# Two transformer blocks with a 32-expert mixture on one core: x read by tiles, weight splits issued at other places, and expert transfers cut in pieces at both ends of the experts

## The reference

```python
for l in range(2):                                   # block 1
    proj = rms_norm(x, norm_mix_pre[l]) @ w_in[l]    # 12 slices of 256 columns
    y = [conformer conv (31 taps), stick-breaking attention, retention, short gated conv]
    x = x + rms_norm(concat(y) @ w_out[l], norm_mix_post[l])
    x = x + rms_norm(conv_ffn(rms_norm(x, norm_ffn_pre[l]), ffn_up[l], ffn_conv_w[l], ffn_down[l]), ...)

mod = silu(c) @ ada_w + ada_b                        # block 2: shifts, scales and gates
u, uc = modulate(rmsnorm(x, norm1_g), ...), modulate(rmsnorm(ctx, norm1_g), ...)
y = token mixer of u, uc: chunked mLSTM (4 heads) and differential attention (8 heads),
    gated branches w_branch_a, w_branch_b, then w_out
x = x + g1 * y
v = modulate(rmsnorm(x, norm2_g), sh2, sc2)
top 4 of softmax(v @ router_w + router_b) over 32 experts; expert e of its tokens:
    h = v @ w1[e] + b1[e]                            # 1024 -> 2048
    a = min(h_glu, 7) * sigmoid(1.702 * ...) * (clip(h_lin, -7, 7) + 1)
    out = a @ w2[e] + b2[e]                          # 1024 -> 1024, summed with the gates
return rmsnorm(x + g2 * sum, final_norm_g)
```

## Time and profile before

| | |
|---|---|
| median of 3 runs | 2085.42 us (2079.37 to 2086.78) |
| the profiled execution | 2082.96 us, span 2081.1 us |
| granted clock, mean | 0.984 |
| PE busy | 1992.8 us, 96% of the span |
| DVE, ACT, POOL busy | 902.9, 633.2, 10.1 us |
| HBM read | 587.27 MB |
| chain that ended last | PE 78%, DMA 14%, DVE 4%, ACT 3%, issue 1% |

### The profile page before, as it was taken

One profiled execution on the slowest core, in us unless ns is written; L12 is line 12 of the kernel. 1 busy time (PEld: TensorE's weight loads), 2 busy tenths in 40 slices (PEclk: granted clock), 3 DMA queues, 4 the chain that ended last, 5 costly groups with the idle time before them and its releaser, 6 DMA issues.

```text
span 2081.1 us, 26818 instructions
## 1 busy us (share of the span) xinstructions
PE 1992.8 (96%) x11078; PEld 1292.9 (62%) x11078; DVE 902.9 (43%) x1552; ACT 633.2 (30%) x1074; POOL 10.1 (0%) x23
## 2 busy tenths in 40 slices
PE   7999999999998999999899999999999999999998
PEld 7969998959996777777798333333333333333332
DVE  6867677867766237456655211111111111111112
ACT  5455556555556324345544100000000000000001
POOL 0000000010000000000000000000000000000000
PEclk9999999999999999999999999999999999999999
DMA  7335544445546544021356999999999999999996
GB/s 304 122 142 197 189 169 167 154 158 212 193 162 263 241 163 173 31 106 57 134 176 250 414 401 432 431 433 433 431 431 431 432 431 433 431 432 431 431 431 278
DMA packets 43211, 589.63 MB, mean 283 GB/s; under 512 B 5200, under 2 KB 5904, under 8 KB 9808
## 3 DMA queue, kind: packets, MB, share of 16 engines
q1 hardware_dynamic: 41392, 583.09, 68.5%
q0 software_dynamic: 1440, 5.01, 0.7%
q10 hardware_dynamic: 288, 0.24, 0.1%
HBM read 587.27 MB, written 1.05 MB: 283 GB/s over the span
## 4 chain that ended last, share of the span: by engine, by line
PE 78%; DMA 14%; DVE 4%; ACT 3%; issue 1%; DVEq 0%; SPq 0%; POOL 0%; ACTq 0%; POOLq 0%
PE psum L2039 46%; PE psum L2492 24%; DMA work<-exp_w_dram 7%; DMA slots<-exp_w_dram 6%; PE psum L2437 3%; PE psum L2609 3%; PE psum L2533 1%; DMA work<-exp_b_dram 1%; DVE work L1406 0%; PE psum L2547 0%; ACT work L927 0%; ACT work L948 0%; DVE work L1688 0%; DVE work L1708 0%; DVE split_weights L1564 0%
## 5 line engine op out<-in xcount | busy, mean ns | idle before, releaser
L2492 PE MATMUL psum<-slots,work 128*64 128x512 f32 x2304 | 525.0, 610 | 26.5 <-DMA slots<-exp_w_dram 14.8
L2039 PE MATMUL psum<-split_rows,split_weights 128*128 128x256 f32 (+1 forms) x3744 | 495.8, 294 | 18.6 <-DVE split_weights L1564 6.9
L2039 PEld LDWEIGHTS psum<-split_rows,split_weights 128*128 128x128 f32 x3744 | 477.1, 194 | 40.5 <-issue 11.0
L2492 PEld LDWEIGHTS psum<-slots,work 128*64 128x64 f32 x2304 | 166.5, 140 | 351.0 <-issue 336.2
L1370 DVE TENSOR_TENSOR split_weights<-slots,split_weights 128x1024 fp32r<-128x1024 f32 x180 | 219.6, 1224 | 132.6 <-ACT split_weights L971 131.7
L971 ACT ACTIVATE split_weights<-slots 128x1024 fp32r<-128x1024 f32 x180 | 190.2, 1060 | 185.7 <-PE psum L2039 166.8
L2039 PE MATMUL psum<-split_weights,split_rows 128*128 128x512 f32 x1008 | 233.1, 391 | 0.0
L2039 PEld LDWEIGHTS psum<-split_weights,split_rows 128*128 128x128 f32 x1008 | 188.3, 188 | 41.8 <-issue 3.3
L2003 DVE TENSOR_SCALAR work<-psum 128x512 f32<-128x512 f32 x32 | 22.0, 688 | 412.4 <-PE psum L2492 412.4
L2492 PE MATMUL psum<-work 128*64 128x512 f32 x768 | 169.4, 593 | 8.6 <-DMA work<-exp_w_dram 8.6
L1278 ACT ACTIVATE work<-work 128x512 f32<-128x512 f32 x32 | 20.2, 631 | 493.7 <-DVE work L2003 493.7
(11 more groups left out here) (273 smaller groups left out, 1409.4 us busy)
## 6 DMA issues: line engine op xcount, KB each, us to landing
slots<-exp_w_dram SPq DMA_DIRECT2D x71, 4096.0 KB, 26.9
work<-exp_w_dram SPq DMA_DIRECT2D x24, 4096.0 KB, 29.7
slots<-w_in_dram SPq DMA_DIRECT2D x56, 1024.0 KB, 6.1
slots<-ffn_up_dram SPq DMA_DIRECT2D x44, 1024.0 KB, 4.8
slots<-ada_w_dram SPq DMA_DIRECT2D x24, 1024.0 KB, 8.8
slots<-ffn_down_dram SPq DMA_DIRECT2D x20, 1024.0 KB, 4.8
slots<-w_out_dram SPq DMA_DIRECT2D x12, 1024.0 KB, 4.8
slots<-w_branch_a_dram SPq DMA_DIRECT2D x4, 1024.0 KB, 5.6
```

Of the source, the lines that this page charges most:

```text
L2039: return nc.tensor.matmul(out_, lhsT, rhs, start=first, stop=last)
L2492: return nc.tensor.matmul(b[rows, :], lhs[:, rows], rhs, start=first, stop=last, skip_group_check=True)
```

## The change

It has six parts.

- **Opening.** x comes in two DMAs, a tile each, with a semaphore each. ACT loads the table for Sqrt ahead of x by a one-element instruction. Only unit 0 is split before the rows; units 1 and 2 behind them. DVE no longer waits for x.
- **Taps.** The split of the 31 taps is 20 + 6 + 5.
- **Block 2's opening.** Two units are split before the loop over q, the third after q = 3 (before: one, and one after q = 1 and q = 3). PE takes the two units together, row by row.
- **mLSTM's last head.** `m_outputs(3)` is issued inside the first `dv` slot: of unit 0's four token tiles, tiles 2 and 3 come first, then `m_outputs(3)`, then tiles 0 and 1.
- **Last attention head.** ACT splits one unit before `head_rows(7)`, one behind it and one after the root; DVE splits one more before it waits for the roots.
- **Experts.** In pair 0 DVE copies G1 before `count_passes` and the b2 scaling. The buffers of places 2 and 3 are swapped, slot n = 2 waits for the last split only, slot n = 4 comes in two halves, the first of which waits for half of slot 0. In pair 15 slot n = 3 goes in two pieces, n = 4 and n = 5 in four each, and PE goes through them by rows.

The core of the diff:

```diff
-            at = 4 * HALF * (s_ - (s_ > 1))
+            at = 4 * HALF * {0: 0, 2: 2, 3: 1}[s_]
...
-            sp.dma_start(x, w["x"].rearrange("b (t p) d -> p (b t) d", p=P)).then_inc(x_loaded, 16)
+            for t in range(TT):
+                sp.dma_start(x[:, t, :], w["x"][0, t * P:(t + 1) * P, :]).then_inc(x_tile_loaded[t], 16)
...
+                    if part == "first" and n == 2:
+                        sp.wait_ge(w_split, DEPTH * len(UNITS) + len(B2_UNITS))
+                    elif part == "first" and n == 4:
+                        to, src = (v.rearrange("p (x h n) -> p x h n", x=2, h=2) for v in (to, src))
+                        sp.wait_ge(first_half_free, 1)
+                        sp.dma_start(to[:, :, 0, :], src[:, :, 0, :]).then_inc(first_half_loaded, 16)
+                        sp.wait_ge(expert_slot_free, 6 * it + (n + 1))
+                        sp.dma_start(to[:, :, 1, :], src[:, :, 1, :]).then_inc(loaded, 16)
+                        continue
+                    else:
+                        sp.wait_ge(expert_slot_free, 6 * it + (n + 1))
+                    if part == "last" and n >= 3:
+                        n_k = 2 if n == 3 else 4
...
-                    act.wait_ge(x_loaded, 16)
-                    rms_of_x(l, lambda t: None)
-                    split_until(UNIT_BUFFERS - 1)
+                    act.wait_ge(zeros_ready, 1)
+                    nc.scalar.activation(stats[:, 46:47], siluc[:, 0, 0:1], ACT.Sqrt)
+                    rms_of_x(l, lambda t: act.wait_ge(x_tile_loaded[t], 16))
+                    split_until(0)
                 act.wait_ge(mix_cols_loaded, 16 * l + 16)
                 high_rows("T", l, 0, COL_MIX_PRE)
+                if l == 0:
+                    split_until(UNIT_BUFFERS - 1)
...
-                split_until(0)
+                split_until(1)
...
-                    if q in (1, 3):
-                        split_until((q + 1) // 2)
+                    if q == 3:
+                        split_until(2)
...
                     out_of(h)
+                    if h == NHD - 1:
+                        split_until(ITEM_UNIT["pa", 1])
                     head_rows(h)
+                split_until(ITEM_UNIT["pa", 1] + 1)
                 load_root_table()
                 head_square(NHD - 1)
                 nc.scalar.activation(b_rms, b_sq, ACT.Sqrt, bias=EPS, scale=1.0 / P).then_inc(head_rms_ready, 1)
+                split_until(ITEM_UNIT["pa", 1] + 2)
...
-                conf_taps(20, 25)
+                conf_taps(20, 26)
...
-                conf_taps(25, CONF_K)
+                conf_taps(26, CONF_K)
...
-                split_until(ITEM_UNIT["pa", 1] + 1)
+                split_until(ITEM_UNIT["pa", 1] + 2)
                 dve.wait_ge(head_rms_ready, 2)
...
+                        order = list(enumerate(tiles))
+                        if j == 0 and within_first:
+                            order = order[2:] + order[:2]
+                        for i, st in order:
+                            if j == 0 and within_first and i == 0:
+                                within_first()
...
+                        by_rows = q == 3 and part == "last"
+                        wt = expert_slot(pe, it, odd, q, 2, not by_rows)
...
-                        by_rows = q == 1 and part == "last"
+                        by_rows = part == "last"
```

More of the change, by code:

```diff
@@ L2144, in second, with column_units_by_rows, column_unit @@
                 u_split = [uT_split[:, v] for v in (0, 1)]
[L2146 removed]
+                def column_units_by_rows(b, kind, s):
+                    units = []
+                    for k in range(KC):
+                        if k % 2 == 0:
+                            pe.wait_ge(u_ready, k // 2 + 1)
+                        for c in (0, 1):
+                            if k == 0:
+                                units.append(next_unit(kind, s, c))
+                            for i, (a, v) in enumerate(PASSES):
+                                ins = nc.tensor.matmul(b[:, c * T:(c + 1) * T], units[c][a][:, k, :], u_split[v][:, k, T:],
+                                                       start=k + c + i == 0, stop=k == KC - 1 and i == 2,
+                                                       skip_group_check=True)
+                            if k == KC - 1:
+                                ins.then_inc(filled[bank_of((kind, 2 * s))] if c else unit_used, 1)
+                def column_unit(b, kind, s, j, t0, rows=u_split):
                     wu = next_unit(kind, s, j)
                     for k in range(KC):
[L2150 to L2151 removed]
                         for i, (a, v) in enumerate(PASSES):
@@ L2524, in pair @@
                                     ins.then_inc(expert_slot_free, 1)
+                                elif part == "first" and xx and (q, k, i) == (0, 0, 3):
+                                    ins.then_inc(first_half_free, 1)
                         if q == 0 and part == "first":
```

68 lines of the change are left out of this document (37 added, 31 removed).

## The result

The changed kernel takes 2066.2 us (median of 4 runs, 2062.86 to 2067.58). In the same comparison the kernel before takes 2084.57. The ratio is 0.9914, interval 0.9896 to 0.9933, so the change gains 18.4 us. Forecast was 2066.0. The profiled execution took 2067.58 us, span 2065.6 us.

The account below looks back on a forecast made before the run. PE's work and waits bound the layers and block 2, then the expert-weight stream at 431 to 433 GB/s. Seven terms summed to 18.1 off the profiled 2082.96, giving 2064.9; allowing for the median, 2066 was forecast, range 2056 to 2076.

Parts of the forecast that it names:

- Opening, 3.3: Kernel start: fewer splits ahead of the rows let PE start near 13.8 instead of 17.17; gain 3.3 us, 2.3 to 3.6.
- Taps, 1.6: Taps of two layers: two of twelve L1406 go ahead, PE waits 0.8 less, twice; gain 1.6 us, 0 to 1.6.
- Block 2's opening, 0.3: Start of block 2: unit 1's split leaves the loop of q, unit 3's stays behind the rows; gain 0.3 us, 0 to 0.4.
- mLSTM's last head, 2.8: First dv slot: 12 matmuls of its first unit fill PE's 3.83 wait; gain 2.8 us, 2.0 to 4.5.
- Last attention head, 5.5: pa and pb units: earlier splits remove waits of 2.31 and 2.64, leaving 0.35; gain 5.5 us, 3.6 to 5.9.
- First pair, 1.9: First expert pair: PE's 1.89 wait for G1's copies goes, early loads count nothing; gain 1.9 us, 1.5 to 1.9.
- Last pair, 2.7: Last expert pair: slots cut in pieces let PE start n = 4 at its first piece; gain 2.7 us, 0.9 to 3.5.
- The next wait takes it: Rival: late splits at opening, dv slot and last attention head pass delays on; 12.3 gained in sum, 2071; chance 0.12.

Follow-up runs that it names:

- r2: The changed kernel with the opening and the taps as before, x in one DMA: 2071.5 us, ratio 0.9949.
- r5: The kernel before with only the splits behind the last attention head moved: 2076.84 us against 2082.84, ratio 0.997.
- r6: The kernel before with only m_outputs(3) moved inside the first dv slot: 2076.89 us, ratio 0.9969.
- r12: The changed kernel with block 2's opening as before, PE going unit by unit: 2062.71 us, ratio 0.9904.
- again: The changed kernel run a second time with no edit: 2065.47 us, ratio to the kernel before 0.992.
- r3: The changed kernel without the first pair's early loads, places 2 and 3 as before, G1's copies still ahead: 2066.32 us, ratio 0.992.
- r11: The changed kernel with the copies of G1 behind count_passes and the b2 scaling, as before: 2071.2 us, ratio 0.9944.
- r7: The kernel before with only the last pair's slots n = 3 to 5 in pieces and by rows: 2083.55 us against 2082.84, ratio 1.0005.
- r10: The changed kernel with unit 3 split after q = 4, count_passes ahead of G1, and the last pair as in the kernel before: 2057.61 us.
- r8: The changed kernel with unit 3 split after q = 4 and count_passes ahead of the copies of G1: 2056.69 us, ratio 0.9874.

## Why the prediction was right, and where it was not

The forecast rested on the claim that PE's waits ahead of the stream count in full, and that the stream's length is fixed. Both held within the spread: r2 and r5 give 6.0 in the time for 6.2 on PE's timeline, r6 6.0 (4 to 9) for 4.4, and the stream is 807 to 808 us in every profile. Term by term:

- **Opening, 3.3.** The mechanism was right, the size a little low: 3.9 at the first unit, 4.6 behind it. The weights landed at 9.2 and not 9.7, and the stretch at half clock, which I had left in my 0.129 for a matmul, was gone.
- **Taps, 1.6.** Right: 0.79, twice. r2 puts both parts together at 6.0 against 4.9.
- **Block 2's opening, 0.3.** Wrong: no gain, and likely a loss (r12). The step that failed is "only ACT's and DVE's split of unit 1 leaves the loop of q": I asked when unit 3 would start, which was right (36.1 behind the second ada product in "again", 36.3 before), and not what the same idle time does when it is gathered into one wait. The clock is at 0.50 behind that wait, and unit 3 takes 1.4 to 2.4 longer than the 3.14 of r12.
- **mLSTM's last head, 2.8.** Undersized. The filled wait was right, and the upper end of my range, the clock, is what happened: 4.4 in the profile, 6.0 by r6's medians with an interval of 4 to 9.
- **Last attention head, 5.5.** 6.2 in the profile, 6.0 in r5. I had 0.35 for the wait that stays (0.54), and 3.11 for a unit that runs at 2.94 in a longer row (11.76 for 96).
- **First pair, 1.9.** The wait for G1 went, and one of 0.55 for L1985 came in: `count_passes` empties a bank that PE needs, which I had not looked for. Net 1.3. The same part held an error that cost nothing: I held that early loads bring nothing, which r3 confirms, but took them to be free. They delay b2's rows by 2.2 (r11). Without the move on DVE the first w1 slot takes 13.4 from start to start instead of the 9.4 of the kernel before: 4 us.
- **Last pair, 2.7.** Wrong: between -0.7 and 0.9 (r7, r10). The two steps that failed: I took the 1.7 that the clock cost in one execution as a constant of the kernel, and I put n = 3 by rows down as a delay that the pieces would more than make up; with it PE waits 1.37 for ACT instead of 0.69. The 0.6 that I had for the price of the pieces is within what the runs show: no more than 0.8 for four more transfers over the whole stream. By the 341 GB/s that the Trainium skill (DMA: Bandwidth & Descriptors, "Measured") gives for a 1 MB transfer, the end would have come 2.6 later than that, an estimate; the runs do not bear this out for pieces queued behind one another. Its rule to batch asks for 1 MiB or more, which the pieces of 1 MiB just meet: what speaks against them there is the figure alone.

The terms that were low (1.3 + 1.6 + 0.7 = 3.6) and those that were high (the last pair by 2 to 3, block 2's opening by 1 or more, the first pair by 0.6) nearly cancel, and the rest is within the spread of the runs. In the two profiled executions the slow load cost the changed kernel some 3 more, and the kernel before's own clock stretch at the end gave back 1.7. That the total came within 0.2 of the measured median is luck: a right total is no proof of its parts.

The clock term of the last heads bears on a rule of the Trainium skill (TensorE: Matmul & The Clock Gate, "The HAM clock gate"), that an idle array falls to 1.2 GHz. The rows agree for the long waits: behind the gathered wait of 5.49 the granted clock is 0.50, and where m_outputs' wait fell from 3.83 to 1.13 its matmuls ran in 6.30 instead of 7.99. For shorter ones the rows do not tell beforehand which wait is followed by a fall. Behind the wait of 2.31 for `pa`'s unit 3 the clock stayed at 1.00 in the kernel before (48 matmuls in 6.05), and fell to 0.50 behind the same 2.31 in r6 (7.42); in r12 it fell among waits of 1.05 and 1.26.

None of the rivals decided. "The next wait takes it" was true at one place only, L1985. What stays open: why the load of block 2's opening is slow in some executions, and in which of them the clock falls behind a wait of 1 to 3 us.

## What to carry to other kernels

Price a stall by what follows it as well as by its length. On this kernel, filling a wait of 3.8 returned another 1.7 in every profile. A stretch at half clock cost little where PE had to wait for rows anyway, and 1.4 to 2.4 us where nothing else held PE. Before a term is built on one profile, ask whether a part of it (a clock stretch, a slow transfer) is there in every execution; the tail's 2.7 was not, and the 1.5 us that seemed lost behind pair 0 were a short stretch in the one profile of the kernel before. And when a change starts a large transfer earlier, look for the small one that someone waits for beside it.

## What the runs showed of the hardware

The same load of 1 MB took 7.4 to 7.9 us in four of fourteen profiles and 5.2 to 5.3 in the others; in one microsecond of a slow one the DMA engines are shown busy (1.10) at 172 GB/s. The stream of expert weights held 431 GB/s and the same 807 to 808 us whether its last three slots came as six or as ten transfers. A load of 128 KB on another queue landed after 13.9 to 15.9 us where two expert slots were issued early beside it, and after 12.7 to 13.3 where they were not.

The best kernel of this case is r8: 2056.69 us, ratio 0.9874 (0.9859 to 0.9889), 9 us below the changed one. It splits unit 3 after q = 4. Where unit 3 stays late, the two units by rows may be worth undoing as well (r12, likely but not shown); with unit 3 early this was not tried.
